# First attention's queries from bfloat16 parts, with half of the index projection moved between the index scores

## The reference, cut to what matters

```python
xa, za, q, k, v, zb, qi, ki, wi, ga, gb = jnp.split(h @ w_in, IN_SPLITS, axis=-1)
s = jax.nn.relu(jnp.einsum('bqhd,bkd->bqhk', qib, k_idx32)) * IDX_SCALE   # 8 index heads of 64
score = jnp.einsum('bqh,bqhk->bqk', wb, s)
score = jnp.where(causal[None], score, -jnp.inf)
_, sel = lax.top_k(score, top_k)                                          # top_k = 256
logits = jnp.einsum('bqhd,bqkd->bqhk', qb, k_sel) * attn_scale            # the queries q enter only here
```

## Time and profile before

| | |
|---|---|
| median of 3 runs | 1923.71 us (1923.46 to 1924.4) |
| the profiled execution | 1922.19 us |
| its span, first to last instruction | 1920.0 us |
| TensorE busy | 1868.0 us, 97% |
| VectorE busy | 1086.7 us, 57% |
| ScalarE / GpSimd busy | 762.2 us, 40% / 595.8 us, 31% |
| mean granted TensorE clock | 0.993 of full |

### The profile page before, as it was taken

One profiled execution on the slowest core, in us unless ns is written; L12 is line 12 of the kernel. 1 busy time (PEld: TensorE's weight loads), 2 busy tenths in 40 slices (PEclk: granted clock), 3 DMA queues, 4 the chain that ended last, 5 costly groups with the idle time before them and its releaser, 6 DMA issues.

```text
span 1920.0 us, 27300 instructions
## 1 busy us (share of the span) xinstructions
PE 1868.0 (97%) x10774; PEld 952.5 (50%) x10774; DVE 1086.7 (57%) x2221; ACT 762.2 (40%) x1449; POOL 595.8 (31%) x590
## 2 busy tenths in 40 slices
PE   8999999999999999999999999999999999999898
PEld 5433454555444556444445555544455555554443
DVE  5418889999997768224544777400333323332527
ACT  4413454443213667204222768411343343334500
POOL 0021433662732215769213310321121122013340
PEclk9999999999999999999999999999999999999999
DMA  9010111212421102232301222012011101110302
GB/s 391 1 55 23 55 44 56 77 39 85 177 95 55 45 28 94 110 131 88 131 12 68 99 96 91 1 53 80 1 45 45 45 1 45 45 37 9 132 23 88
DMA packets 22847, 134.31 MB, mean 70 GB/s; under 512 B 2400, under 2 KB 2656, under 8 KB 17600
## 3 DMA queue, kind: packets, MB, share of 16 engines
q1 hardware_dynamic: 18496, 109.01, 15.0%
q0 software_dynamic: 4224, 23.56, 3.1%
HBM read 113.63 MB, written 18.94 MB: 69 GB/s over the span
## 4 chain that ended last, share of the span: by engine, by line
PE 76%; DVE 11%; ACT 5%; DMA 4%; POOL 3%; issue 2%; SPq 0%; DVEq 0%; POOLq 0%; ACTq 0%
PE ps L1084 51%; PE ps L1078 7%; DVE arena L1970 2%; PE ps L1212 2%; PE ps L1189 2%; PE ps L1195 2%; DVE small L2222 1%; DMA hT<-in_mods 1%; DMA W<-in_loads 1%; PE ps L1134 1%; PE ps L1512 1%; PE ps L1354 1%; PE ps L1160 1%; POOL W L760 1%; PE ps L1121 1%
## 5 line engine op out<-in xcount | busy, mean ns | idle before, releaser
L1084 PE MATMUL ps<-hT,W 128*128 128x512 bf16 x3312 | 745.9, 380 | 8.6 <-ACT arena L1615 3.2
L1084 PEld LDWEIGHTS ps<-hT,W 128*128 128x128 bf16 x3312 | 317.9, 98 | 398.5 <-issue 32.4
L760 POOL TENSOR_TENSOR W<-W 128x512 bf16<-128x512 f32 x162 | 175.3, 1122 | 376.1 <-DMA W<-in_loads 276.3
L1084 PE MATMUL ps<-W,arena 128*128 128x512 bf16 x1104 | 245.3, 382 | 0.5 <-DVE small L1970 0.5
L1693 ACT ACTIVATE arena<-arena,small 128x128 f32<-128x128 f32 (+9 forms) x192 | 114.0, 641 | 187.6 <-DVE small L2063 167.0
L1084 PEld LDWEIGHTS ps<-W,arena 128*128 128x128 bf16 x1104 | 108.1, 98 | 133.6 <-issue 2.7
L1686 ACT ACTIVATE arena<-arena,small 128x128 f32<-128x128 f32 (+9 forms) x192 | 122.9, 641 | 117.4 <-DVE small L2052 88.9
L2052 DVE CUSTOM_DVE_ANT_0 arena<-ps,arena 128x256 f32<-128x256 f32 (+7 forms) x128 | 62.1, 518 | 118.1 <-PE ps L1195 104.2
L2222 DVE TENSOR_SCALAR_CACHE_REDUCE small<-arena,small 128x640 bf16<-128x640 f32 (+1 forms) x124 | 126.5, 1077 | 1.1
L1084 PE MATMUL ps<-arena,W 128*128 128x512 bf16 x576 | 125.0, 379 | 1.3 <-ACT arena L1605 1.2
L1078 PE MATMUL ps<-arena,W 128*128 128x512 f32 x256 | 114.7, 599 | 0.0
(11 more groups left out here) (349 smaller groups left out, 2743.0 us busy)
## 6 DMA issues: line engine op xcount, KB each, us to landing
W<-in_loads SPq DMA_DIRECT2D x20, 2048.0 KB, 8.2
W<-in_loads SPq DMA_DIRECT2D x13, 1792.0 KB, 7.1
gates_scratch<-arena SPq DMA_DIRECT2D x32, 256.0 KB, 2.0
arena<-gates_scratch POOLq DMA_DIRECT2D x2, 4096.0 KB, 14.2
arena<-sums_scratch SPq DMA_DIRECT2D x16, 512.0 KB, 3.6
W<-in_mods SPq DMA_DIRECT2D x2, 2048.0 KB, 17.2
hT<-in_mods SPq DMA_DIRECT2D x2, 2048.0 KB, 21.5
arena<-in_x POOLq DMA_DIRECT2D x1, 4096.0 KB, 14.5
```

The source lines that it names most:

```text
L760: last = nc.gpsimd.tensor_tensor(low(v), v, high(v), ALU.subtract)
L1084: last = mm(o, left[:, :, a], moving, start=(k == 0 and (a, b) == PRODUCTS[0]), stop=(k == steps - 1 and (a, b) == PRODUCTS[-1]))
```

## The change

The queries `q` leave `WHOLE`: their 8 units are made from bfloat16 parts. GpSimd gets `split("q")` ahead of `output_blocks(0)` and of `split("xa")`. The units of the index projection are put in a new order: first the four of the first 512 tokens (`qi` 0, 2, 4, 6), and the scores of tiles 2 and 3, which need only those, begin after them (`AT_SCORES`). The four units of the later tokens (`LATER_ORDER`) become fillers of pairs 0 to 7, `q`'s of pairs 8 to 19, with two shares after pairs 9, 12, 15 and 18, and `xa`'s of pairs 20 to 23 as before. Ahead of tile 4 TensorE waits until all `qi` units are copied out and the low part of `h` is there.

```diff
FIRST_ORDER = [("small", 0), ("small", 2), ("qi", 0), ("qi", 2), ("small", 1), ("small", 3), ("small", 4), ("small", 5),
-               ("qi", 1), ("qi", 3)]
+               ("qi", 4), ("qi", 6)]
+LATER_ORDER = [("qi", 1), ("qi", 3), ("qi", 5), ("qi", 7)]
+AT_SCORES = len(FIRST_ORDER)
...
-    units[0:len(FIRST_ORDER)] = FIRST_ORDER
+    units[0:14] = FIRST_ORDER + LATER_ORDER
...
-WHOLE = {"small", "qi", "q", "gate0", "gate1"}
+WHOLE = {"small", "qi", "gate0", "gate1"}
...
+def index_fillers():
+
+    later = range(AT_SCORES, FIRST["xa"] + 2)
+    shares = [(u, share) for u in later for share in (0, 1)]
+    made = []
+    for pair in range(24):
+        take = 2 if 8 <= pair < 20 and pair % 3 == 0 else 1
+        made.append(shares[:take])
+        shares = shares[take:]
+    assert not shares
+    return made
...
-    if UNITS[u][0] in ("q", "zs0", "zs1"):
+    if UNITS[u][0] in ("q", "zs0", "zs1") or UNITS[u] in LATER_ORDER:
         return u % 2
...
+INDEX_FILLERS = index_fillers()
...
+            split("q")
+            output_blocks(0)
             split("xa")
-            output_blocks(0)
             split("za")
...
-            for u in range(4, unit_end("qi")):
+            for u in range(4, AT_SCORES):
                 unit(u)
 
-            pe.wait_ge(s_free, unit_end("qi"))
+            pe.wait_ge(s_free, AT_SCORES)
             n = 0
             for i in range(2, NT):
+                if i == NT // 2:
+                    pe.wait_ge(s_free, unit_end("qi"))
+                    pe.wait_ge(s_hlow, KD)
                 for j in range(HEADS1 // 2):
...
-                    pair = n // 2
-                    if pair < 20 and pair % 5 < 4:
-                        unit(FIRST["q"] + pair // 5 * 2 + pair % 5 // 2, pair % 5 % 2)
-                    if pair >= 20:
-                        if pair == 20:
-                            pe.wait_ge(s_hlow, KD)
-                        unit(FIRST["xa"] + (pair - 20) // 2, pair % 2)
+                    for u, share in INDEX_FILLERS[n // 2]:
+                        unit(u, share)
                     n += 2
...
-            for u in range(3, unit_end("qi")):
+            for u in range(3, AT_SCORES):
                 evac(u)
...
-                if n < 40 and n % 2 and n // 2 % 5 in (1, 3):
-                    evac(FIRST["q"] + n // 10 * 2 + n // 2 % 5 // 2)
+                if n % 2:
+                    for u, share in INDEX_FILLERS[n // 2]:
+                        if share == 1 and u < FIRST["xa"]:
+                            evac(u)
```

## The result

The changed kernel took 1902.38 us (median of 4 runs, 1901.61 to 1903.31), the kernel before 1924.06 us (4 runs, 1923.46 to 1924.79) on the same chip: a ratio of 0.9887, 95% interval 0.987 to 0.9904. That is 21.7 us faster. The profiled execution took 1901.66 us, 20.5 us less than the one of before.

A forecast was written before the change was run, and what follows sets the result against it. TensorE was taken to bound the scores, and `q`'s end the state-space stage. The turns' 14.5 us less 1.7 for the clock gave 12.8 us gain, 1909.4 us profiled, 1910.9 us as median; range 1906.5 to 1916.

The forecast's parts named there:

- rival 2: Scores: VectorE or the coupling slows, score products wait for relus; gain only 5 to 10 us, time 1916.5 us; chance 0.12.
- rival 5: Tiles 4 to 6: alternating float32 and bfloat16 products lower the clock, 1971 us; chance 0.04 together with other losses.
- What I costed at nothing: Ahead of and during the scores: splits of `q` and `xa`, ScalarE's copies, SyncE's stores and VectorE's work add no time.
- the split of `za`, 14.5 us: From `q`'s end to the first rotation: GpSimd's shorter split lets the turns come 14.5 us earlier, within 14.2 to 15.9.
- The rival estimate from the Trainium skill: Split of `za`: two pieces run at full speed wherever VectorE runs the top-k, giving about 15.5 us instead of 14.5.
- So a like idle time costs about 1.7 us: At the state inputs: TensorE's idle time grows to about 2.7 us, the clock falls, and 1.7 us are lost.
- Rival 1: At the state inputs: the clock doesn't fall in the new idle time; 14.5 us gain, 1909.2 us; chance 0.28.
- From there every row should lie 12.8 to 14.5 us earlier to the end: Behind the first rotation: its lead of 12.8 to 14.5 us carries unchanged to the kernel's end.
- VectorE and TensorE run in step ... Nothing there has slack: Behind the start of the state-space stage: both engines nearly fully busy from 303 to 367 us, so all follows the first rotation.

The follow-up runs named there:

- the run with the heads first: Changed kernel with a wait added on GpSimd, so the split of `za` begins only after the last index head; 1912.22 us, ratio 0.9952.
- the repeats: The changed kernel run twice more without edit, each beside the kernel before on the same chip; 1904.15 us (0.9911) and 1903.48 us (0.9904).
- the parts alone: Kernel before with `q` made from bfloat16 parts, order and fillers as before; 1910.29 us, ratio 0.9946.
- four rounds moved: Changed kernel with four of VectorE's top-k rounds moved from the second batch to ahead of the first rotation; 1902.27 us (three runs), ratio 0.9903.
- 6 + 2 pieces: Changed kernel with top-k rounds dealt 12, 7, 13, 0 and the last two of eight pieces of `za`'s split behind the first turns; 1898.43 us, ratio 0.9877.

## Why the prediction was wrong

**Right: up to the end of `q`.** Start of the scores 94.36 (94.6), `q`'s end 192.41 (192.5), TensorE 17.07 us earlier in tile 7 (17.0), the split's begin 202.31 (201.9). No waits for relus (rival 2's stalls) and no fall of the clock in the scores (rival 5: 1.00 in both windows above). What I costed at nothing was hidden: the split of `q` from 65.40 took 14.22 us and the one of `xa` from 139.45 took 9.78, each done long before its first use.

**Wrong in size: the split of `za`, 14.5 us.** I had bounded the turns' gain at 14.2 to 15.9 us and chosen near the lower end, because VectorE has two-input work behind its last head. It measured 16.0, just above the upper bound. The slower pieces beside heads are real (8.99 us behind the heads, 12.34 across their end, 14.37 and 14.57 with heads beside nearly all of it), but the work that I feared, the block placing, began at 214.89, after the split. The wrong step was to carry the mean of 1.82 us a piece over to the new schedule. Piece by piece, one takes 2.02 us beside a head and 1.04 in a pause of VectorE: in the kernel before six of eight took 2.02, in the changed one four. VectorE's pauses between the heads of tile 7 are 1.92 and 1.95 us now and were shorter before, where its first head of the tile began 5.3 us behind TensorE's first scores of it (now 3.6). Before:

```profile
217.18 3.66 DVE L2261 SCALAR_TENSOR_TENSOR arena<-arena 128x1024 f32<-128x1024 f32 x2 [0.30 <-ACT arena L1765]
221.80 4.00 DVE L2261 SCALAR_TENSOR_TENSOR arena<-arena 128x1024 f32<-128x1024 f32 x2 [0.96 <-ACT arena L1765]
```

Only the last piece, 1.09 us, lay behind the last head. The rival estimate from the Trainium skill (SBUF — State Buffer, section Who interferes with whom), 15.5 us, was nearer in its number, but it too was reckoned from two such pieces and not from the pauses. The split is 1.5 us of the 3.1 that were missing at the rotation.

**Wrong: "So a like idle time costs about 1.7 us".** This is the other half of those 3.1 us, and the step failed twice. The idle time was 0.99 us, since TensorE arrived 16.7 us earlier and not 17.0, and the copies 15.9 and not 14.5. And a like idle time, 2.75 us in the run with the heads first, left the products at full speed. The size was right elsewhere (7.04 against 5.36 us, 1.7 us). Rival 1, the clock doesn't fall, was the case that came in, though its time, 1909.2 us, was far off as well; my own argument for it, 48 dense products ahead, fits the 2.75 us, but no run separates it from chance.

**Wrong, and the step that carried the time out of the range: "From there every row should lie 12.8 to 14.5 us earlier to the end".** With both terms above right, the sum would have been some 1907.8 us as a median, still inside. But the lead stayed constant only to 415 us, then grew by 4.6 us, from 15.9 to 20.5, where the sum had nothing. The growth is made of a different wait for the stores of the gates (0.9 us net), one of TensorE at 505 us (1.35), 0.6 near 885 and the clock near 1805 (1.8). The first and the last vary between executions of the same kernel. The wait at 505 us doesn't look like chance: the three profiles with `q` in float32 have it (0.9 to 1.2 us), all eleven with bfloat16 parts lack it, and the split of `zb`, for which the copy waits by way of GpSimd, then begins 16.5 to 17.0 us behind its load instead of 17.8 to 18.0. Why, I can't say; no run took it apart. With 15.9 us from the rotation, some 1.35 from this wait and the rest uncertain, the repeats' 17.3 and 18.2 us are the fairer size of the gain; the 21.7 us of the first comparison hold some luck of both kernels. Measured as a gain, the range of the forecast ended at 17.2 us.

**"VectorE and TensorE run in step ... Nothing there has slack"** was half right. TensorE has none, VectorE had the idle time ahead of the first rotation and could give 6 us away up to 340 us without moving a product.

## What to carry to other kernels

Cheaper work on one engine pays fully only if its neighbour gets its own work early enough: here 11 us for the cheaper products alone, nothing for the order alone, 17 to 18 for both. When a term has bounds, look at which instructions really stand in the disputed interval in the shifted schedule before choosing an end, and don't carry over a mean that holds pauses of the old schedule. A gain of 1% here is read to 1 us only from several executions, since one kernel's own profiles differ by 3.5 us. Don't count a fall of the clock behind an idle time as certain; count it as a chance, and rather look for the waits that cause such idle times, since taking one away can give back wait and clock together.

## What the runs showed of the hardware

Idle time alone didn't decide whether TensorE's granted clock fell to 0.50 (1.2 GHz): it fell after 1.74 us (at 910 us, heads first), 2.29, 2.76, 3.20, 3.38 and 4.17 us, and stayed at 1.00 after 2.75, after 3.42 (at 359 us, the parts alone) and after 3.47 us. The last is a place where it fell in the first profile of the same kernel. That kernel has a second such place: behind 2.64 us at 1132.87 it fell, behind 2.68 us in the other profile it stayed. This row, then the fall behind 2.29 us, with four rounds moved, and a window behind the one after 2.76 us, with the parts alone:

```profile
1131.60 5.35 PE L1084 MATMUL ps<-W,hT 128*128 128x512 bf16 x24 [2.68 <-ACT arena L1642]
...
351.12 7.04 PE L1103 MATMUL ps<-hT,W 128*128 128x512 bf16 x24 [2.29 <-ACT arena L1632]
...
176.30:179.00 2.70, 2.70 (x8) 1.10 (x8) 2.60 (x6) 0.81 (x1) 0.00 (x0) 0.50 0.00 0
```

The contention between GpSimd and VectorE goes both ways: a piece of GpSimd's split took 2.02 us beside a head of VectorE and 1.04 in its pauses, and two 128x256 products of VectorE went from 0.76 us to 3.18 and 4.04 beside GpSimd's two-input multiplication. They took 1.48 us beside the beginning of one of its one-input steps (6 + 2 pieces), so these can cost VectorE time too.
